# Output projection of a hybrid encoder: the first two token tiles multiplied side by side, with the loop over weight tiles outside

## The reference, cut to what matters

```
mixed = concatenate([o_mla * silu(gate_mla), o_pool * silu(gate_pool), o_gla * silu(gate_gla)], axis=-1)
x = x + einsum('bse,ed->bsd', mixed, w_out)          # w_out: 1024 x 1024
y = x * rsqrt(mean(x * x) + 1e-6) * final_norm_g
```

## Time and profile before

| | |
|---|---|
| time, median of 3 runs | 901.8 us (901.74 to 901.93) |
| the profiled execution | 899.46 us, span 897.7 us |
| TensorE busy over the span | 786.3 us (88%) |
| mean granted TensorE clock | 0.953 of full |
| output stage | from 741.6 us to the end of the span |

### The profile page before, as it was taken

One profiled execution on the slowest core, in us unless ns is written; L12 is line 12 of the kernel. 1 busy time (PEld: TensorE's weight loads), 2 busy tenths in 40 slices (PEclk: granted clock), 3 DMA queues, 4 the chain that ended last, 5 costly groups with the idle time before them and its releaser, 6 DMA issues. The chain is left out here.

```text
span 897.7 us, 14265 instructions
## 1 busy us (share of the span) xinstructions
PE 786.3 (88%) x5936; PEld 649.4 (72%) x5936; DVE 410.9 (46%) x665; ACT 346.5 (39%) x582; POOL 193.5 (22%) x211
## 2 busy tenths in 40 slices
PE   3999795995999999999873589999999983999996
PEld 2786683774788888888763478888788872788885
DVE  5722685322544442100067256666766766343332
ACT  6433521453534452221142154444444545232221
POOL 2221130423833532121024000000000006232220
PEclk9999897997999999999968699999999997999999
DMA  6410001201111111121053300000006003254431
GB/s 260 126 35 31 34 29 43 71 3 60 60 49 61 48 61 49 48 97 44 12 166 103 78 12 14 24 12 13 12 13 223 1 1 118 68 171 153 145 129 60
DMA packets 32442, 61.36 MB, mean 68 GB/s; under 512 B 3296, under 2 KB 16000, under 8 KB 32384
## 3 DMA queue, kind: packets, MB, share of 16 engines
q1 hardware_dynamic: 29840, 52.66, 17.9%
q10 hardware_dynamic: 2544, 7.87, 2.2%
HBM read 42.42 MB, written 17.69 MB: 67 GB/s over the span
## 5 line engine op out<-in xcount | busy, mean ns | idle before, releaser
L77 PE MATMUL psum<-h_hi,z_w_hi 128*128 128x512 f32 x432 | 178.4, 413 | 8.9 <-ACT z L384 5.1
L78 PE MATMUL psum<-h_lo,z_w_hi 128*128 128x512 f32 x432 | 170.6, 395 | 0.0
L79 PE MATMUL psum<-h_hi,z_w_lo 128*128 128x512 f32 x432 | 170.6, 395 | 0.0
L77 PEld LDWEIGHTS psum<-h_hi,z_w_hi 128*128 128x128 f32 x432 | 82.5, 191 | 31.0 <-issue 8.8
L79 PEld LDWEIGHTS psum<-h_hi,z_w_lo 128*128 128x128 f32 x432 | 82.3, 191 | 18.3
L78 PEld LDWEIGHTS psum<-h_lo,z_w_hi 128*128 128x128 f32 x432 | 82.8, 192 | 16.7 <-issue 1.0
L1551 ACT ACTIVATE a_weights<-psum,a_bias,mla_q_scale 128x1024 f32<-128x1024 f32 (+1 forms) x48 | 51.1, 1065 | 103.9 <-DVE a_bias L1590 103.9
L77 PE MATMUL psum<-o_w_hi,o_m_hi 128*128 128x512 f32 x192 | 76.7, 400 | 14.9 <-DVE o_w_lo L1878 14.4
L78 PE MATMUL psum<-o_w_lo,o_m_hi 128*128 128x512 f32 x192 | 75.8, 395 | 0.0
L79 PE MATMUL psum<-o_w_hi,o_m_lo 128*128 128x512 f32 x192 | 75.7, 394 | 0.0
L1614 DVE TENSOR_TENSOR a_turned_lo<-psum,a_turned_hi 128x512 fp32r<-128x512 f32 x80 | 52.3, 687 | 41.7 <-ACT a_turned_hi L1568 41.7
(11 more groups left out here) (209 smaller groups left out, 1522.7 us busy)
## 6 DMA issues: line engine op xcount, KB each, us to landing
z_w_raw<-in_w_z_dram SPq DMA_DIRECT2D x17, 512.0 KB, 3.5
n_x_in<-in_x_dram SPq DMA_DIRECT2D x12, 512.0 KB, 4.1
gates_scratch<-z_gate SPq DMA_DIRECT2D x24, 256.0 KB, 2.0
o_x_in<-in_x_dram SPq DMA_DIRECT2D x12, 512.0 KB, 3.6
out_dram<-o_y ACTq DMA_DIRECT2D x12, 512.0 KB, 2.6
o_w_raw<-in_w_out_dram SPq DMA_DIRECT2D x8, 512.0 KB, 9.4
a_q_rope<-rope_scratch SPq DMA_DIRECT2D x12, 256.0 KB, 2.6
o_gate_first<-gates_scratch SPq DMA_DIRECT2D x6, 512.0 KB, 5.0
```

The lines of the kernel that those rows point to most:

```text
L77: nc.tensor.matmul(out, a_hi, b_hi, start=first, stop=False)
L78: nc.tensor.matmul(out, a_hi, b_lo, start=False, stop=False)
L79: return nc.tensor.matmul(out, a_lo, b_hi, start=False, stop=last)
```

## The change

For tiles 0 and 1 TensorE no longer takes one half after another. `multiply_first(s, part)` goes through four weight tiles (part 0 is k 0 to 3, part 1 is k 4 to 7), and for each of them through both halves. The four calls run in the order tile 0 part 0, tile 1 part 0, tile 0 part 1, tile 1 part 1. Each waits for one more `m_lo` part. The other engines prepare tile 1 earlier. GpSimd weights its gate ahead of `w_lo[4]`, ScalarE opens it ahead of `w_hi[1]` and makes `m_hi` of it ahead of `w_hi[6]`, and VectorE makes `w_lo[0]` ahead of `m_lo` of tile 0, and `m_lo` of tile 1 ahead of `w_lo[5]`. SyncE's code and the loop from tile 2 on stay as they are.

```diff
             weight_gates(0, 0)
             for k in range(1, KT, 3):
+                if k == 4:
+                    weight_gates(0, 1)
                 pool.wait_ge(w_hi_ready, k + 1)
...
-            weight_gates(0, 1)
             with pool.Fori(0, pairs - 1) as i:
...
                 act.wait_ge(w_loaded[k], 16)
+                if k == 1:
+                    open_gate(0, 1)
                 if k == 2:
                     take_hi(0, 0, True)
-                if k == 4:
-                    open_gate(0, 1)
+                if k == 6:
+                    take_hi(0, 1, True)
                 nc.scalar.activation(w_hi[:, k, :], w_raw[:, k, :], ACT.Copy).then_inc(w_hi_ready, 1)
-            take_hi(0, 1, True)
...
-            take_lo(0, 0)
             for k in range(KT):
+                if k == 2:
+                    take_lo(0, 0)
+                if k == 5:
+                    take_lo(0, 1)
                 if k % 3 != 1:
...
-            take_lo(0, 1)
...
+            def multiply_first(s, part):
+                pe.wait_ge(m_lo_ready, 2 * s + 1 + part)
+                for k in range(4 * part, 4 * part + 4):
+                    if s == 0:
+                        if k % 3 == 1:
+                            pe.wait_ge(w_lo_pool, k // 3 + 1)
+                        else:
+                            pe.wait_ge(w_lo_ready, k + 1 - (k + 1) // 3)
+                    for half in range(2):
+                        mm = product(nc, psum[:, 2 * s + half, :], m_hi[:, s, k, :], m_lo[:, s, k, :],
+                                     w_hi[:, k, half * BLK:(half + 1) * BLK], w_lo[:, k, half * BLK:(half + 1) * BLK],
+                                     k == 0, k == KT - 1)
+                        if k == KT - 1:
+                            mm.then_inc(out_mm, 1)
...
-            for s in range(2):
-                multiply(0, s, True)
+            for part in range(2):
+                for s in range(2):
+                    multiply_first(s, part)
```

More of the change, by code:

```diff
@@ L1896, in _, with multiply @@
         def _(pe):
-            def multiply(i, s, first):
+            def multiply_first(s, part):
[12 more added lines that the diff above has]
+                            mm.then_inc(out_mm, 1)
+            def multiply(i, s):
                 n = 2 * i + s
@@ L1900, in multiply @@
                 for half in range(2):
-                    if not first:
-                        pe.wait_ge(summed, 2 * n - 3 + half)
+                    pe.wait_ge(summed, 2 * n - 3 + half)
                     cols = slice(half * BLK, (half + 1) * BLK)
                     for k in range(KT):
[L1905 to L1909, removed]
                         mm = product(nc, psum[:, 2 * s + half, :], m_hi[:, s, k, :], m_lo[:, s, k, :],
@@ L1912, in multiply @@
                     mm.then_inc(out_mm, 1)
-            for s in range(2):
-                multiply(0, s, True)
+            for part in range(2):
+                for s in range(2):
+                    multiply_first(s, part)
             with pe.Fori(1, pairs) as i:
                 for s in range(2):
-                    multiply(i, s, False)
+                    multiply(i, s)
 class Semaphores:
```

## The result

The changed kernel takes 904.29 us in the median of 7 runs (903.33 to 905.90), the kernel before 901.68 in 7 runs beside it (899.57 to 901.93). The ratio is 1.0037, with a 95% interval of 1.0027 to 1.0047: 3.3 us slower, 2.4 to 4.2. The forecast was 905.2 and +3.4.

A forecast was written before the change was run, and what follows sets the result against it. Tile 2's start bounds the kernel, since TensorE is busy from there on. Tile 0's later completion (+1.86) and the slow clock (+1.55) give +3.4 us on the median: 905.2 us, 8-in-10 range 903.0 to 907.6.

The forecast's parts named there:

- Turns: Output stage's preparation: VectorE and GpSimd run one at a time, alternating; first matmul at 750.57, 0.74 us earlier.
- The 96 matmuls sooner: Tiles 0 and 1 on TensorE: all 96 matmuls issued by 776.8 instead of 780.38, 3.6 us sooner.
- Tile 0 later: Tile 0 completes after 72 matmuls instead of 48, so tile 2 can start 1.86 us later.
- The clock: After the roughly 6 us pause before tile 2, TensorE starts at half clock, costing 1.55 us.
- The prediction's upper value, 2.7: Clock cost at tile 2 if the return to full clock takes half as long again: 2.7 us.
- the early slow clock: Rival: clock already falls in the early gaps before tile 1, a second slow stretch; +5.0 us, 906.8; 16%.
- Little or no change: Rival: early waits vanish (+0.3) or the clock survives the pause cheaply (+1.9); 902.1 to 903.7 us; 15%.
- Faster: Rival: tile 2 directly follows tile 1, keeping the 3.6 us; needs a chain of at most 5.7 us; 898.2; 4%.

The follow-up runs named there:

- E1: Changed kernel with SyncE issuing both gate loads of a pair before both input loads; ratio 0.9952 to the kernel before.
- E4: Kernel before with only TensorE's order changed: weight tiles outside, both halves inside, all of tile 0 and then tile 1; ratio 0.9946 to the kernel before.
- E3: Changed kernel with 25 extra, unused matmuls filling the pause between tile 1 and tile 2; ratio 1.0025 to the kernel before.
- E8: Changed kernel run again without edits, in the same job as E9; median 905.99 us, ratio 1.0062 to the kernel before.
- E9: E3 run again beside E8: changed kernel with 25 extra matmuls in the pause; median 903.78 us, ratio 1.0034 to the kernel before.
- E6: Changed kernel with all eight `w_lo` on VectorE, GpSimd only weighting the gates; ratio 1.0016 to the kernel before.
- E7: Kernel before with TensorE's order of E4, gate loads first as in E1, and all `w_lo` on VectorE; median 893.82 us, ratio 0.9920.

## Why the prediction was right

By its steps, in stage times:

- **Turns.** The first matmul was forecast 8.93 us into the stage (750.57 less 741.64), measured 8.83. The wait before tile 1 was to end at 18.93, measured 18.88. Up to there the worked-out schedule, twelve instructions in turn, was right to 0.1 us. (One step, GpSimd's `w_lo[1]` to 749.88, should by its own terms read 749.80.) Behind it one turn fell otherwise: GpSimd issued its next gating only at 762.53, just before VectorE's next start, and `m_lo` part 1 of tile 1 went first, not second. It held nothing up.
- **The 96 matmuls sooner.** Forecast at 35.2 (776.8 less 741.64), measured 35.15 (778.95 less 743.80): the 3.6 us were really won. The prediction does not say what they are made of. The earlier start gives 0.84 (9.67 against 8.83) and the shorter waits 1.14 (3.51 against 2.37). The largest part, 1.6 us, is a second slow stretch that the kernel before has from 761.2 on and the changed one has not:

```profile
763.94 0.63 PE L77 MATMUL psum<-o_w_hi,o_m_hi 128*128 128x512 f32 x1
764.37 0.54 PE L78 MATMUL psum<-o_w_lo,o_m_hi 128*128 128x512 f32 x1
764.74 0.39 PE L79 MATMUL psum<-o_w_hi,o_m_lo 128*128 128x512 f32 x1
```

  From 761.22 to 764.74 the kernel before takes 3.52 us for eight spacings, against 1.92 at full clock. So the change trades a slow stretch among the early waits for one behind the pause.
- **Tile 0 later.** Tile 2 was forecast at 41.5, measured 41.52, so +1.92 against before. E1 and E4 show it from both sides: free the chain, or complete tile 0 earlier, and the loss becomes a gain.
- **The clock.** Right in kind and too small in size: the term was 1.55, and the profile's rows and E3 show 2.3 to 2.4. It was read from the first return of the clock in the kernel before, where seven spacings were slow; here it was eleven and part of a twelfth. The prediction's upper value, 2.7, has no working behind it: a return half as long again as 3.36 us costs about 2.3 by its own terms, which is what came. With 1.92 and 2.31 the sum is +4.2, which the stage shows (+4.24).
- **The time.** That the median, +3.3, lies 0.1 from the forecast +3.4 is luck: the mechanism as measured in the stage gives +4.2, and in the job of E8 and E9 the changed kernel was 5.6 us slower (4.3 to 6.9). The two intervals barely miss each other. Why the same pair of kernels lies 3.3 us apart in one job and 5.6 in another was not settled. Some 0.6 of it shows in the stage (+4.83 in E8), where the gate transfer of tile 3 took 5.05 us from its issue to the opening, against 4.73. The start of the stage varies by more: 743.06 and 741.03 in E3 and E9, which are one kernel.

Of the rivals, the early slow clock did not happen (full clock from 756.2 to 783.5). "Little or no change" fell with both its premises, since the early waits stayed and the clock did fall in the pause. "Faster" named the right condition, a chain of no more than 5.7 us: once E1 had brought it to 5.2 the kernel was faster by 4.3 us.

## What to carry to other kernels

Before reordering a busy engine's work, find what its products release: here tile 0's sums released a transfer that tile 2 needed, and finishing two tiles together delayed the first of them by 1.9 us although the pair was done 3.6 us sooner. A queue that issues loads in program order ties each load to every wait written ahead of it, so write the waits that come true early first. And a pause costs TensorE more than its length: idling of 5.9 to 6.3 us cost another 2.1 to 2.4 at half clock in the three kernels that had it (E6, the changed kernel, E8).

## What was not expected of the hardware

- Who comes next between VectorE and GpSimd is not always the one that waits. In E6 a gating of GpSimd, issued at 758.18, stayed out through three `w_lo` of VectorE in a row and ended 1.15 us behind them. In all turns of the kernel before it had waited for one instruction at most.

```profile
758.18 4.64 POOL L1759 TENSOR_TENSOR mla_mixed<-mla_mixed,o_gate_first 128x512 f32 x1 [5.61 <-ACT o_gate_first L1790]
```

```profile
758.19 3.48 DVE L1877 TENSOR_TENSOR o_w_lo<-o_w_raw,o_w_hi 128x1024 fp32r<-128x1024 f32 x3
```

  In E7 the same gating, issued at 759.94 while VectorE was in a `w_lo`, got in after that one and took 2.17 us. The changed kernel has a third case, in which a gating let one instruction pass:

```profile
762.53 1.85 POOL L1759 TENSOR_TENSOR mla_mixed<-mla_mixed,o_gate_first 128x512 f32 x1 [0.39 <-POOL o_eps L1772]
```

```profile
759.76 2.87 DVE L1853 TENSOR_TENSOR o_m_lo<-mla_mixed,o_m_hi 128x512 fp32r<-128x512 f32 x1
762.55 0.68 DVE L1856 TENSOR_TENSOR o_m_lo<-z,o_m_hi 128x512 fp32r<-128x512 f32 x1
```

  There and in E6 the gating was issued only 0.1 us before VectorE's running instruction ended (762.63 and 758.27), in E7 1.0 us before. That may be why one passed; why three did in E6 is open.
- The return to full clock varied, though TensorE had no gap within any of these stretches: from the first matmul of the stage it took six slow spacings in E4, seven in the kernel before and eleven in E7, and behind the pause eleven in the changed kernel and twelve in E8.
